# Sums of squares and gate gaps moved to GpSimd, fewer small products and waits, in a hybrid decoder layer

## What is computed

```python
h = rmsnorm(x, g_pre_mix)
z, q, k, v, glow, og = split(h @ w_in)
gk = log_sigmoid(glow @ w_gk2 + b_gk2) / 16
pool_out = (window_mean(z, 2|4|8|16) - z) @ w_pool * pool_scale
# gated linear attention, 4 heads, key 64, value 128:
#   S_t = diag(exp(gk_t)) S_{t-1} + k_t^T v_t ;  o_t = q_t S_t
gla_out = rmsnorm(o, gla_norm) * silu(og)
x = x + rmsnorm(concat(pool_out, gla_out) @ w_o, g_post_mix)
f = gelu(conv3(rmsnorm(x, g_pre_ffn) @ w_up_gate)) * (... @ w_up) @ w_down
x = x + rmsnorm(f, g_post_ffn)
x = x + (p @ w_ple) * sigmoid(x @ w_ple_gate)
```

## Time and profile before

| | us |
|---|---|
| median of 3 runs (2678.04 to 2681.24) | 2680.86 |
| the profiled execution | 2677.16 |
| its span, first to last instruction | 2675.40 |
| TensorE busy | 2614.0 |
| VectorE busy | 1716.3 |
| ScalarE busy | 1363.5 |
| GpSimd busy | 262.0 |

### The profile page before, as it was taken

The page is one execution under the profiler, slowest core; times in us unless marked ns, Lnnn a source line. Parts: engine busy times, 40 slices in busy tenths (PEclk is TensorE's granted clock), DMA queues, the critical chain, the costliest instruction groups (busy, mean ns, idle before and its releaser), DMA issues.

```text
span 2675.4 us, 41472 instructions
## 1 busy us (share of the span) xinstructions
PE 2614.0 (98%) x16662; PEld 2535.7 (95%) x16662; DVE 1716.3 (64%) x2547; ACT 1363.5 (51%) x2164; POOL 262.0 (10%) x545
## 2 busy tenths in 40 slices
PE   7989999999999999999999999999999999999998
PEld 6979999999999999999999999999999999899997
DVE  5667756666665675666567566656756664767865
ACT  4445554555444455544445554444555444466554
POOL 2200101100000110000011000001100000111000
PEclk9989999999999999999999999999999999999999
DMA  4235444234434323444432344443234444334563
GB/s 135 74 106 173 151 133 127 87 111 146 150 122 122 109 80 116 143 150 124 122 108 82 116 142 150 124 122 107 87 111 144 143 127 122 122 134 168 187 181 130
DMA packets 101588, 340.46 MB, mean 127 GB/s; under 512 B 10478, under 2 KB 18710, under 8 KB 101398
## 3 DMA queue, kind: packets, MB, share of 16 engines
q1 hardware_dynamic: 101398, 337.81, 39.2%
HBM read 327.46 MB, written 10.31 MB: 126 GB/s over the span
## 4 chain that ended last, share of the span: by engine, by line
PE 88%; DVE 5%; ACT 3%; DMA 2%; issue 1%; POOL 1%; POOLq 0%; DVEq 0%; ACTq 0%
PE G L1553 27%; PE G L1555 26%; PE G L1554 26%; PE X L1606 2%; DVE ffn_out L1376 1%; PE X L1549 1%; PE X L1546 1%; DVE w_lo L1091 1%; ACT w_hi L689 1%; DVE mixed L1302 1%; DMA stage<-in_w_in_units_dram 1%; PE X L1678 1%; PE X L1663 1%; DMA stage<-in_w_up_units_dram 1%; PE X L1681 1%
## 5 line engine op out<-in xcount | busy, mean ns | idle before, releaser
L1553 PE MATMUL G<-h_hi,w_hi 128*128 128x384 f32 (+2 forms) x3264 | 1070.0, 328 | 21.7 <-DVE w_lo L1091 10.1
L1554 PE MATMUL G<-h_hi,w_lo 128*128 128x384 f32 (+2 forms) x3264 | 1054.1, 323 | 0.0
L1555 PE MATMUL G<-h_lo,w_hi 128*128 128x384 f32 (+2 forms) x3264 | 1054.0, 323 | 0.0
L689 ACT ACTIVATE w_hi<-stage 128x1024 fp32r<-128x1024 f32 (+1 forms) x612 | 637.2, 1042 | 738.2 <-DMA stage<-in_w_up_units_dram 279.4
L1091 DVE TENSOR_TENSOR w_lo<-stage,w_hi 128x1024 fp32r<-128x1024 f32 (+1 forms) x612 | 746.6, 1221 | 133.3 <-ACT w_hi L689 132.9
L1553 PEld LDWEIGHTS G<-h_hi,w_hi 128*128 128x128 f32 x3264 | 619.3, 190 | 32.0 <-issue 13.2
L1554 PEld LDWEIGHTS G<-h_hi,w_lo 128*128 128x128 f32 x3264 | 619.6, 190 | 2.1 <-issue 0.6
L1555 PEld LDWEIGHTS G<-h_lo,w_hi 128*128 128x128 f32 x3264 | 619.3, 190 | 0.0
L1553 PE MATMUL G<-y_hi,w_hi 128*128 128x384 f32 (+2 forms) x1056 | 346.5, 328 | 0.0
L1555 PE MATMUL G<-y_lo,w_hi 128*128 128x384 f32 (+2 forms) x1056 | 339.9, 322 | 0.0
L1554 PE MATMUL G<-y_hi,w_lo 128*128 128x384 f32 (+2 forms) x1056 | 339.4, 321 | 0.0
(11 more groups left out here) (220 smaller groups left out, 2695.5 us busy)
## 6 DMA issues: line engine op xcount, KB each, us to landing
stage<-in_w_up_units_dram SPq DMA_DIRECT2D x264, 512.0 KB, 3.5
stage<-in_w_in_units_dram SPq DMA_DIRECT2D x96, 512.0 KB, 3.5
stage<-in_w_down_units_dram SPq DMA_DIRECT2D x96, 448.0 KB, 3.3
stage<-in_w_o_units_dram SPq DMA_DIRECT2D x48, 512.0 KB, 3.5
stage<-in_w_down_units_dram SPq DMA_DIRECT2D x48, 512.0 KB, 3.5
stage<-in_w_gate_units_dram SPq DMA_DIRECT2D x48, 512.0 KB, 3.5
x_tok<-in_x_prompt_dram SPq DMA_DIRECT2D x16, 512.0 KB, 5.4
stage<-in_w_ple_units_dram SPq DMA_DIRECT2D x12, 512.0 KB, 3.4
```

The source lines that it names most:

```text
L689: act.activation(w_hi[s][:, 0:parts, :], stage[s][:, 0:parts, :], ACT.Copy).then_inc(hi_made, 1)
L1553: pe.matmul(ps[:, 0:w], l_hi, r_hi[:, 0:w], start=start, stop=False)
L1554: pe.matmul(ps[:, 0:w], l_lo, r_hi[:, 0:w], start=False, stop=False)
L1555: return pe.matmul(ps[:, 0:w], l_hi, r_lo[:, 0:w], start=False, stop=stop)
```

## The change

GpSimd makes all seven gaps of a tile, in its stream behind the additions of the previous tile's output; from the third level on it waits for the operands of two levels earlier. GpSimd also adds the eight squares for the "up" root into one tile (`add_f`, `f_added`), and TensorE makes a single product with ones from it, behind the first "up" unit. The diagonal is made for both heads at once, with a constant of two columns (`of_head`) that GpSimd builds at the start. `out_chunk` has its 64-row products in one run. ScalarE empties a bank before it makes the next w_hi. The norms of the down results, the splits of x, and the turning and copying of y are spread over other units.

The diff, without most of the lines of context and with twelve columns of indentation removed:

```diff
@@ -48,7 +48,7 @@
 X_LAST_POOL = (1, 3, 5, 7)
-BUILT = 9 + 3 + 4 * len(LEVELS) + 3 + (1 + 1) + (1 + 3) + (1 + 7) + (1 + 15)
+BUILT = 9 + 3 + 3 + 4 * len(LEVELS) + 3 + (1 + 1) + (1 + 3) + (1 + 7) + (1 + 15)
@@ -185,6 +185,7 @@
         of_seq = own("of_seq", [NS, NSEQ])
+        of_head = own("of_head", [P, 2])
@@ -351,7 +352,7 @@
         f_hi_made, f_lo_made = signal("f_hi_made", KD), signal("f_lo_made", KD)
-        f_squared, f_summed, f_rooted = signal("f_squared", KD), signal("f_summed", KD), signal("f_rooted")
+        f_squared, f_added, f_summed, f_rooted = signal("f_squared", KD), signal("f_added", KD - 1), signal("f_summed"), signal("f_rooted")
@@ -574,6 +575,9 @@
     build(pool.tensor_copy(masks[:, n_level, :], sel[:, 0:64]))
+build(pool.memset(of_head[:, :], 0.0))
+for b in range(2):
+    build(pool.memset(of_head[64 * b:64 * b + 64, b:b + 1], 1.0))
@@ -605,6 +609,14 @@
     pool.wait_ge(*cum_made.at(t, 1))
+    for n, h in enumerate(LEVELS):
+        if n >= 2:
+            pool.wait_ge(*operands.at(t, n - 2))
+        v = level_whole(cum, h, t)
+        mid = v[:, :, :, h - 1:h].broadcast_to(list(v.shape))
+        gap_made.did(pool.tensor_tensor(level_whole(gap[n % 2], h, t), v, mid, ALU.subtract), t, n)
@@ -641,10 +653,25 @@
-    for m in POOL_MIXED:
+    def add_mixed(m):
                                           mixed[:, m, 0:width(t)], ALU.add), t, POOL_MIXED.index(m))
+    def add_f(m):
+        pool.wait_ge(*f_squared.at(t, m))
+        if m > 1:
+            pool.wait_ge(*f_added.at(t, m - 2))
+        f_added.did(pool.tensor_tensor(total[:, 0:width(t)], total[:, 0:width(t)], sq[:, m % 2, 0:width(t)],
+                                       ALU.add), t, m - 1)
+    add_mixed(1)
+    add_mixed(3)
+    add_f(1)
+    add_f(2)
+    add_mixed(5)
+    for m in range(3, KD):
+        add_f(m)
@@ -827,12 +854,10 @@
     f_hi_made.did(act.activation(h_hi[:, m, 0:w], xr[t % 2][:, m, 0:w], ACT.Copy, scale=gains[:, 2, m:m + 1]), t, m)
-    if m >= 2:
-        act.wait_ge(*f_summed.at(t, m - 2))
-    f_squared.did(act.activation(sq[:, m % 2, 0:w], xr[t % 2][:, m, 0:w], ACT.Square), t, m)
+    square(xr[t % 2][:, m, :], sq, total, t, m, f_squared, f_added)
 def root_f(t):
-    act.wait_ge(*f_summed.at(t, KD - 1))
+    act.wait_ge(*f_summed.at(t))
@@ -941,13 +966,13 @@
 for n, (t, kind, m) in enumerate(UNITS):
-    make_hi(n + 2)
         finish(n - 1)
+    make_hi(n + 2)
@@ -955,9 +980,9 @@
             decay(t, m - 3)
-        if 2 <= m <= 5 and t:
-            x_split(t - 1, 2 * m - 4)
-            x_split(t - 1, 2 * m - 3)
+        if 3 <= m <= 6 and t:
+            x_split(t - 1, 2 * m - 6)
+            x_split(t - 1, 2 * m - 5)
@@ -990,15 +1015,11 @@
             head_split(u, h)
-    if kind == "gate" and t < LAST:
-        if m == 2:
-            copy_y(t, 0)
-        if m > EARLY_GATES:
-            if m > EARLY_GATES + 1:
-                copy_y(t, m - 2)
+    if kind == "gate" and t < LAST and m >= EARLY_GATES + 3:
+        copy_y(t, m - 3)
     if kind == "o":
-        if t and m in (0, 1):
-            copy_y(t - 1, m + 1)
+        if t and m < 3:
+            copy_y(t - 1, m)
@@ -1022,12 +1043,12 @@
             else:
-                copy_y(t - 1, KD - 2)
+                copy_y(t - 1, KD - 3)
             act.preload_act_table(ACT.Gelu_apprx_tanh)
-        if m == 1 and t:
-            copy_y(t - 1, KD - 1)
+        if m in (1, 2) and t:
+            copy_y(t - 1, KD - 3 + m)
@@ -1143,14 +1164,6 @@
-def make_gap(t, n):
-    if n == 0:
-        dve.wait_ge(*cum_made.at(t, 1))
-    h = LEVELS[n]
-    v = level_whole(cum, h, t)
-    mid = v[:, :, :, h - 1:h].broadcast_to(list(v.shape))
-    gap_made.did(dve.tensor_tensor(level_whole(gap[n % 2], h, t), v, mid, ALU.subtract), t, n)
@@ -1175,12 +1188,13 @@
     dve.wait_ge(*diag_made.at(t))
+    sums = X[2][:, 0:2 * (nc_ + 2)].rearrange("p (r b) -> p b r", b=2)
     for b in range(2):
-        diag = X[2 + b][:, 0:nc_].unsqueeze(2).broadcast_to([P, nc_, P])
+        diag = sums[:, b, 0:nc_].unsqueeze(2).broadcast_to([P, nc_, P])
         if small(t):
-            diag = X[2 + b][0:NS, nc_:nc_ + 2].unsqueeze(2).broadcast_to([NS, 2, NS])
+            diag = sums[0:NS, b, nc_:nc_ + 2].unsqueeze(2).broadcast_to([NS, 2, NS])
@@ -1412,29 +1426,24 @@
             add_d(t - 1, KD - 1)
-        if m in (1, 2) and t:
-            for k in range(4 * m - 4, 4 * m):
-                norm_ffn(t - 1, k)
                 p_rest(t - 1, k)
+        if m in (1, 2, 3) and t:
+            for k in ((0, 1), (2, 3), (4, 5, 6, 7))[m - 1]:
+                norm_ffn(t - 1, k)
             make_qk(t)
+        if 4 <= m <= 10:
+            make_operand(t, m - 4)
             take_scores(t, m - 5)
-        if 3 <= m <= 9:
-            make_gap(t, m - 3)
             chunk_gap(t)
-        if 4 <= m <= 10:
-            make_operand(t, m - 4)
             decayed_kq(t)
-        if m in (3, 12) and t:
-            for k in range(2) if m == 3 else range(2, KD):
-                x_rest(t - 1, k)
@@ -1443,6 +1452,9 @@
             make_u(t, 2 * m - 27)
+        if m in (12, 14, 15) and t:
+            for k in {12: (0, 1, 2, 3), 14: (4, 5), 15: (6, 7)}[m]:
+                x_rest(t - 1, k)
@@ -1614,20 +1626,16 @@
     nc_, np_ = chunks(t), prompt(t)
-    for b in range(2):
-        take(2 + b, diag_taken.at(t))
+    take(2, diag_taken.at(t))
         for c in range(nc_):
-            for b in range(2):
-                r, col = head_rows(b), d * nc_ + c
-                last = pe.matmul(X[2 + b][:, col:col + 1], opnd[1][r, d, cols(c)], ones[r, 0:1],
-                                 start=True, stop=True)
+            col = 2 * (d * nc_ + c)
+            last = pe.matmul(X[2][:, col:col + 2], opnd[1][:, d, cols(c)], of_head[:, :], start=True, stop=True)
         if small(t):
-            for b in range(2):
-                r, col = head_rows(b), 2 * nc_ + d
-                last = pe.matmul(X[2 + b][0:NS, col:col + 1], opnd[1][r, d, np_:np_ + NS], ones[r, 0:1],
-                                 start=True, stop=True)
+            col = 2 * (2 * nc_ + d)
+            last = pe.matmul(X[2][0:NS, col:col + 2], opnd[1][:, d, np_:np_ + NS], of_head[:, :],
+                             start=True, stop=True)
@@ -1673,13 +1681,21 @@
         pe.wait_ge(*state_made.at(t, c - 1))
-    for d in range(2):
+    def inside(d, start):
         for b in range(2):
-            pe.matmul(X[first + b][:, cols(d)], v_tok[:, c, cols(2 * d + b)], A[:, b, d * chunks(t) + c, :],
-                      start=True, stop=False)
+            last = pe.matmul(X[first + b][:, cols(d)], v_tok[:, c, cols(2 * d + b)],
+                             A[:, b, d * chunks(t) + c, :], start=start, stop=not start)
+        return last
+    def before(d, start):
         for b in range(2):
-            last = pe.matmul(X[first + b][:, cols(d)], S[head_rows(b), state_no(t, c), d, :],
-                             qT[head_rows(b), d, cols(c)], start=False, stop=True)
+            pe.matmul(X[first + b][:, cols(d)], S[head_rows(b), state_no(t, c), d, :],
+                      qT[head_rows(b), d, cols(c)], start=start, stop=not start)
+    inside(0, True)
+    before(0, False)
+    before(1, True)
+    last = inside(1, False)
@@ -1737,11 +1753,10 @@
-def sum_f(t, m):
-    if m == 0:
-        take(3, f_rooted.at(t))
-    pe.wait_ge(*f_squared.at(t, m))
-    f_summed.did(ones_sum(X[3], sq[:, m % 2, :], t, m == 0, m == KD - 1), t, m)
+def sum_f(t):
+    take(3, f_rooted.at(t))
+    pe.wait_ge(*f_added.at(t, KD - 2))
+    f_summed.did(ones_sum(X[3], total, t), t)
@@ -1874,17 +1887,14 @@
                 pool_group(t + 1, 3)
-            if m not in (0, EARLY_GATES):
-                turn_y(t, m - 1)
-            if m >= EARLY_GATES:
-                for k in ((0, 1), (2, 3), (4, 5), (6,), (7,))[m - EARLY_GATES]:
-                    sum_f(t + 1, k)
+            if m == EARLY_GATES - 1 or m >= EARLY_GATES + 2:
+                turn_y(t, m - 2)
         whole_unit(n, h_hi, h_lo, None if m else mix_lo_made)
-        if t and m == 0:
-            turn_y(t - 1, EARLY_GATES - 1)
+        if t and m < 2:
+            turn_y(t - 1, EARLY_GATES - 2 + m)
@@ -1897,11 +1907,11 @@
             sum_o(t)
-            whole_unit(n, h_hi, h_lo, f_lo_made, sum_f)
-        else:
-            whole_unit(n, h_hi, h_lo, None if m else f_lo_made)
-        if m == 0 and t:
-            turn_y(t - 1, KD - 1)
+        whole_unit(n, h_hi, h_lo, None if m else f_lo_made)
+        if m == 0:
+            sum_f(t)
+        if m in (0, 1) and t:
+            turn_y(t - 1, KD - 2 + m)
```

More of the change, by code:

```diff
@@ L1770, in turn_y, with whole_unit @@
                 y_turned.did(last, t, m)
-            def whole_unit(n, hi, lo, ready=None, between=None):
+            def whole_unit(n, hi, lo, ready=None):
                 t, kind, m = UNITS[n]
@@ L1782, in whole_unit @@
                         last.then_inc(ticks, 1)
-                    if between:
-                        between(t, k)
```

## The result

| | before | after |
|---|---|---|
| median us (lowest to highest, 5 runs each) | 2678.04 (2674.63 to 2681.24) | 2693.91 (2690.88 to 2699.5) |
| the profiled execution's span | 2675.4 | 2694.4 |
| mean granted clock | 0.989 | 0.977 |

The changed kernel takes 1.0062 times as long, 95% interval 1.005 to 1.0075: slower by 0.6%. I had forecast 2672.

A forecast was written before the change was run, and what follows sets the result against it. It took TensorE, busy 98%, as the bound, limited by what VectorE delivers in time. The terms -8.0 + 1.7 + 1.9 - 0.6 - 1.2 - 3.1 + 2.0 - 1.2 gave -8.5 us: 2672 at the median, range 2650 to 2686.

The forecast's parts named there:

- The first "in" units: First units of each tile, gaps on GpSimd: +1.9 us in all, bounds -10 and +12.
- the sum for the chain: From last norm through first gap to q times k and scores: +0.5 us each for tiles 2 to 4.
- Rival 2: First-gap chain 1 us longer per tile, plus a second low clock stretch: +7 to +12 us, 2680; chance 0.22.
- Tile 0's first "up": Tile 0, where products wait for VectorE: additions on GpSimd and earlier bank emptying, +1.7 us together.
- The chain's +2.4: Tile 0: additions lengthen VectorE's chain and the remaining sum waits for the last one, +2.4 us.
- The late gates: Late gate units: seven of eight sums leave TensorE, additions slow VectorE; -8.0 us, bounds 0 and -21.1.
- The middle tile's 1.6: Late gates, tiles 2 to 4: 2.4 us gained, up to 0.95 given back, so 1.6 us each.
- Small products: Diagonal for both heads at once, -0.6 us in tile 0 only; one row change fewer per output chunk, -1.2 us.
- The turns' own -3.1: Early gates: turning y blocks one unit later removes their sig wait, -3.1 us.
- Start: Kernel start: three more memsets exposed, +0.5 us, and two gaps colliding with h_lo; +2.0 us in all.
- End: Kernel end: ScalarE empties a bank before the w_hi, removing TensorE's wait of 1.16 us; -1.2 us.
- Rival 3: GpSimd gap over 2.5 us, so VectorE and ScalarE can't keep a unit's 5.85 us; 2722 at 4 us; chance 0.07.

The follow-up runs named there:

- e12: The changed kernel with sums of squares back on TensorE and 14 products of constants ahead of the diagonal of tiles 1 to 5: 2675.35 us.
- e10: The changed kernel with gaps back on VectorE, sums back on TensorE, and six products of constants ahead of the diagonal: 2663.53 us.
- e15: The changed kernel with gaps back on VectorE and six products of constants behind parts two, four and five of tile 0's first "up" unit: 2671.24 us.
- e6: The kernel before with one part of the change alone, the sums of squares on GpSimd: 2695.04 us.
- e4: The changed kernel with the eight sums of squares back on TensorE and none on GpSimd: 2684.54 us.
- e2: The changed kernel with 14 products of constants on TensorE ahead of the diagonal of tiles 1 to 5: 2689.68 us.
- e14: The changed kernel with gaps back on VectorE and, in tiles 1 to 4, six products of constants behind the last gate and six before the first "up": 2667.84 us.

## Why the prediction was wrong

**The first "in" units.** Predicted +1.9 in all, measured +17.6 with "in" 5. For the middle tiles the sum for the chain held: I had q times k 25.0 us after the start of "in" 0 and it came at 25.0; I had +0.5 per tile, and with the clock kept up it is +1.2. GpSimd's gap took the 1.5 us that I had put; 1.47 to 1.56 where nothing met it, 2.44 where VectorE did. For tiles 1 and 5 it didn't hold. I had put 0 and -0.9; "in" 0 to 5 with the fill (e12) is 28.5 us in tile 1, for 26.1 (up to 0.5 of it is fill beyond the wait, an estimate from 14 products of 0.18 us, as six took 1.1 in e10, against a wait of 2.04), and 27.6 in tile 5, for 26.1: in tile 5 the w_lo wait of 4.1 us went, and one of 7.8 ahead of the diagonal came. The larger part of the loss, some 10 of the 17.6 us (187.2 less e12's 176.9), is the clock, and there what failed is the sentence after the chain: "Today this ends in a stretch of 3.5 us at a granted clock of 0.51 ... I expect it to stay". I had written down that TensorE would now idle 3 us or more in one piece, and gave that piece no price. It doubled or tripled the stretch (6.8 to 10.2 us in tiles 1 to 4, 13.7 for 6.8 in tile 5), and pulled it forward into the diagonal and the scores, on the path. Rival 2 had the mechanism, but 7 to 12 us for it.

**Tile 0's first "up".** Predicted +1.7, measured +4.0, and 1.3 more at the lower clock in the unit behind (5.05 us for 3.76). The chain's +2.4 is right: VectorE's part runs 15.3 us from its first norm to its last h_lo, 13.1 before. Two operations of VectorE, after, beside GpSimd's additions:

```profile
187.58 1.16 DVE L1316 SCALAR_TENSOR_TENSOR mixed<-mixed,const,rms 128x320 f32<-128x320 f32 x1
188.77 1.03 DVE L1322 TENSOR_TENSOR xr<-xr,mixed 128x320 f32<-128x320 f32 x1
```

They take 0.54 and 0.49 alone. What I missed is that the sums between the parts kept TensorE at work (busy all of 10.4 us before, 8.7 of 14.4 after), and that without them the clock doesn't come back in the unit: 1.0 to 1.5 us (e15). The early emptying (-0.7) didn't show; the "o" units ahead became 1.5 us longer, with 10.1 us at the lower clock for 7.9.

**The late gates.** Predicted -8.0. The middle tile's 1.6 was made of a stage 2.4 shorter and 0.95 given back: measured 1.5 shorter and 0.7 given back, net 0.8. The mechanism was right to a few tenths: I had VectorE's weights for the first "up" unit 4.6 us later, 25.5 us after the stage's start, and they end at 26.3. VectorE's row, after, beside tile 2:

```profile
1082.66 2.02 DVE L1112 TENSOR_TENSOR w_lo<-stage,w_hi 128x1024 fp32r<-128x1024 f32 x1
```

and TensorE's, the last turn before the first "up" unit and that unit's first product:

```profile
1082.89 0.52 PE L1558 MATMUL X<-ident,sig 128*128 128x128 f32 x3 [1.53 <-DVE sig L1410]
1084.74 0.69 PE L1565 MATMUL G<-h_hi,w_hi 128*128 128x384 f32 x1 [1.32 <-DVE w_lo L1112]
```

Tile 1 came out at 0 as put, tile 5 at -3.1 for -3.2. But these two waits are new, and the low clock behind them cost 2.8 and 1.6 us in tiles 2 and 4, which no term had. And two edits were costed as if alone: without the later turns the same sums lose 18 us (e6), and with them TensorE's own sums do as well in tiles 2 to 4 and 1.8 us better in tile 1 (e4).

**Small products.** The diagonal gave nothing: at the full clock (e2, tile 2) 12 instructions take the 1.50 us that 24 took the earlier trace rows. The chunk outputs gave more, -0.39 us per chunk (5.89 us per unit instead of 6.29), 16 chunks, -6.2 for my -1.2. After:

```profile
983.15 0.61 PE L1686 MATMUL X<-A,v_tok 128*128 128x128 f32 x4
983.68 0.72 PE L1692 MATMUL X<-qT,S 64*128 64x128 f32 x8
984.33 0.71 PE L1686 MATMUL X<-A,v_tok 128*128 128x128 f32 x4
```

From the first product to the next unit's it is 1.65 us, and was 2.03. I counted one change of rows less; there are two less (in and out of the second group), and each costs some 0.2 us. "TensorEngine Tiling (Array Packing)" of the Trainium skill (Tiling Modes, Key Properties) says that a change of mode drains the engine. The rows agree in kind; I had sized it from one row on one side of the change.

**Turned blocks, start, end.** The turns' own -3.1 is not there: the stretch from the first "ple" to gate 3 changed by -0.5 (tile 1) to +0.15 us. Start: +1.5 to the end of tile 0's "in" units, for +2.0 and the diagonal's -0.6. End: -0.4 for -1.2; the last gates ran 13.0 us at the lower clock, for 8.4.

How far off would the sum have been without the clock? TensorE was busy in 99.1 us of the low stretches, for 47.0 before: at half speed that is up to 26 us of work lost. Counted by stage it is 17 to 18 (10.3 in the first "in" units, 1.5 and 1.3 in tile 0, 2.8 and 1.6 in the "up" units). So of the profiled execution's 19.0 us the change alone would be between -7 and +2, an estimate, where I had -8.5. That nearness is partly luck: the chains cost 7 us where I had 0.6, the late gates and the turns gave 5.6 for 11.1, and the chunk outputs gave 5 more than I had put. The step that failed is that I treated the clock as a fixed cost of each tile and not as a quantity that the change moves. Rival 3 (a gap of over 2.5 us) was not the one to fear: the longest took 2.44.

## What to carry to other kernels

An instruction taken from an engine that is busy 98% of the time is only a gain where that engine doesn't have to wait instead; look for the rows that will wait, and give the low clock behind each new wait a price of its own. Before moving work to a helper engine, follow that engine's own order to the first result that someone needs, and what stands behind the one who waits for it: here an unrelated bank. Test the parts of a change in pairs: the gaps on GpSimd cost nothing in the kernel before, and 22 us beside the later norms. The rest of the change, with gaps and sums left where they were, is 0.5% faster than before.

## What the runs showed of the hardware

- **A wait of a microsecond can cost as much again in clock.** In the late gates, waits of 1.5 and 1.3 us were followed by up to 6.8 us at 1.2 GHz (in the changed kernel tile 2's "up" 0 and 1 took 2.8 us longer than tile 3's, behind the same waits). With them filled no unit there ran low (e14, one execution), nor in six traces without such waits.
- **It varies from run to run.** One kernel (e2) ran from 2679 to 2698 us, roughly in step with its granted clock, 0.985 to 0.978. The spread comes with the sums on GpSimd and not with the longest wait: with the sums on TensorE ten runs lie within 3.1 us (e4), though TensorE waits 3.8 us ahead of the diagonal in each middle tile.
- **A VectorE operation that meets one of GpSimd takes about twice as long.** At 320 columns VectorE's 0.54 us operation takes 1.15, at 384 columns 0.61 becomes 1.38, and GpSimd's gap of 768 makes a 0.96 us product take 1.82. That much I had put down; that GpSimd's second gap would meet q times k, on the path, I had not.
- **Halving the number of the diagonal's products bought nothing:** 12 over 128 rows with two columns take as long as 24 over 64 rows with one, 0.12 us each for 0.06.
